# A decoder layer on one core: queries in halves, tile 0's convolution beside attention, side work as one even stream over the prompt rows

## The reference, cut to what matters

```python
mod = silu(c) @ w_ada + b_ada            # sh1, sc1, gt1, sh2, sc2, gt2: six pieces of 1024 columns
h   = rms_norm(x, norm1) * (1 + sc1) + sh1
z   = h @ w_in                           # q, three k/v pairs, branch gates, GLU input
o_attn = nsa(z)                          # compressed, selected and window branches, 8 heads
u   = glu_a * sigmoid(glu_b)             # convolution: 31 taps, 512 channels, then LayerNorm, silu
mix = concat(rms_norm(o_attn), conv(u) * scale) @ w_out
x   = x + gt1 * mix
h2  = rms_norm(x, norm2) * (1 + sc2) + sh2
q   = h2 @ peer_q                        # 8 heads x 2 halves x 128
s   = q . sub_keys                       # 128 scores for each head and half
# per head: top 16 of each half, top 16 of their 256 sums -> 16 expert indices and softmax gates
x   = x + gt2 * sum_k gate_k * gelu(h2 . expert_u[idx_k]) * expert_v[idx_k]
```

## Time and profile before

| | us |
|---|---|
| median of 3 runs | 2302.16 |
| lowest, highest | 2285.15, 2314.85 |
| the profiled execution's own time | 2287.22 |
| its span, first to last instruction | 2285.2 |

### The profile page before, as it was taken

One profiled execution on the slowest core, in us unless ns is written; L12 is line 12 of the kernel. 1 busy time (PEld: TensorE's weight loads), 2 busy tenths in 40 slices (PEclk: granted clock), 3 DMA queues, 4 the chain that ended last, 5 costly groups with the idle time before them and its releaser, 6 DMA issues.

```text
span 2285.2 us, 29811 instructions
## 1 busy us (share of the span) xinstructions
PE 1654.6 (72%) x10176; PEld 979.5 (43%) x10176; DVE 1289.0 (56%) x3724; ACT 656.7 (29%) x1676; POOL 604.9 (26%) x548
## 2 busy tenths in 40 slices
PE   7876358896854769877539798879689858769743
PEld 5746324453621435545116445646254514436300
DVE  1641687565388585743887565327766441443655
ACT  2132133273112433811224275112224220231111
POOL 0000133232323323322423233312323211222342
PEclk9787669697967887988769699889798876675665
DMA  7684789998998899989879999986989866798897
GB/s 283 211 324 145 280 351 426 382 405 360 389 412 325 327 416 385 426 328 426 355 323 390 383 393 399 384 305 224 414 321 410 322 248 217 281 381 320 308 416 296
DMA packets 149256, 782.11 MB, mean 342 GB/s; under 512 B 17303, under 2 KB 53047, under 8 KB 59554
## 3 DMA queue, kind: packets, MB, share of 16 engines
q0 software_dynamic: 78336, 570.46, 62.0%
q1 hardware_dynamic: 70771, 209.77, 24.0%
HBM read 773.75 MB, written 10.99 MB: 343 GB/s over the span
## 4 chain that ended last, share of the span: by engine, by line
PE 39%; DVE 26%; DMA 16%; issue 7%; ACT 6%; SPq 5%; POOL 1%; POOLq 0%; ACTq 0%; DVEq 0%
PE bank L994 13%; DMA expert_rows<-in_expert_uv,expert_index 10%; DVE expert_rows L1837 6%; PE bank L825 6%; DVE conv_out L1447 4%; PE bank L696 4%; PE bank L607 3%; PE bank L800 3%; PE bank L872 2%; DMA gate_or_shift_and_scale<-mod_dram 2%; SPq L1909 2%; DMA weight_units<-in_w_ada_units 2%; PE bank L759 1%; DVE stage_room L1647 1%; DVE stage_room L1636 1%
## 5 line engine op out<-in xcount | busy, mean ns | idle before, releaser
L1866 POOL DMA_INDIRECT expert_rows<-in_expert_uv,expert_index x544 | 604.7, 1111 | 1652.8 <-PE bank L994 1250.8
L994 PE MATMUL bank<-expert_rows,weight_diagonals 64*64 64x512 f32 x4096 | 654.4, 768 | 254.0 <-ACT weight_diagonals L1337 208.0
L1837 DVE CUSTOM_DVE_ANT_0 expert_rows<-expert_rows,h_rows 128x1024 f32<-128x1024 f32 x544 | 657.5, 1220 | 205.7 <-DMA expert_rows<-in_expert_uv,expert_index 203.8
L994 PEld LDWEIGHTS bank<-expert_rows,weight_diagonals 64*64 64x64 f32 x4096 | 160.2, 163 | 569.7 <-ACT weight_diagonals L1337 274.3
L1328 ACT ACTIVATE group_gelu<-group_dots 128x2 f32<-128x2 f32 x272 | 55.2, 203 | 764.7 <-DVE group_dots L1837 720.8
L1337 ACT ACTIVATE weight_diagonals<-consts_sb,group_weights 128x64 f32<-128x64 f32 (+1 forms) x544 | 158.3, 338 | 294.1 <-DVE group_weights L1804 285.9
L825 PEld LDWEIGHTS bank<-stage_room,weight_units 128*128 128x128 f32 x1280 | 169.4, 217 | 41.0 <-issue 37.2
L825 PE MATMUL bank<-stage_room,weight_units 128*128 128x128 f32 (+1 forms) x1280 | 176.8, 301 | 2.4 <-ACT stage_room L1224 2.4
L1804 DVE TENSOR_TENSOR group_weights<-group_gelu,expert_gate 128x2 f32<-128x2 f32 x272 | 43.3, 159 | 195.2 <-ACT group_gelu L1328 178.6
L1447 DVE SCALAR_TENSOR_TENSOR conv_out<-stage_room,small_weights,conv_out 128x128 f32<-128x128 f32 (+1 forms) x600 | 150.4, 322 | 0.0
L872 PE MATMUL bank<-weight_units,prompt_bias 128*128 128x256 f32 x512 | 121.9, 395 | 0.0
(11 more groups left out here) (245 smaller groups left out, 1583.2 us busy)
## 6 DMA issues: line engine op xcount, KB each, us to landing
weight_units<-in_w_in_units SPq DMA_DIRECT2D x45, 1024.0 KB
weight_units<-in_peer_q_units SPq DMA_DIRECT2D x40, 1024.0 KB
weight_units<-in_w_ada_units SPq DMA_DIRECT2D x24, 1024.0 KB
weight_units<-in_w_out_units SPq DMA_DIRECT2D x20, 1024.0 KB
weight_units<-in_w_units SPq DMA_DIRECT2D x16, 1024.0 KB
expert_rows<-in_expert_uv,expert_index POOLq DMA_INDIRECT x544
weight_units<-in_cmp_pages SPq DMA_DIRECT2D x128, 64.0 KB
gate_or_shift_and_scale<-mod_dram SPq DMA_DIRECT2D x12, 512.0 KB
```

The source lines that it names most:

```text
L994: last = mm(e.bank[2 * a + c][o * HD:(o + 1) * HD, :], e.diag[ps, m % (NG * GR)], e.ring[ps, m % RING, cs], start=first, stop=final)
L1837: vec.tensor_tensor_reduce(out=row, in0=row, in1=e.h2[:, i % 2], scale=1.0, scalar=0.0, op0=ALU.mult, op1=ALU.add, accum_out=e.dots[:, q % ...
L1866: pool.indirect_dma_start(e.ring[:, n % RING], None, e.io["expert_uv"], bass.IndirectOffsetOnAxis(ap=e.eidx[:, i % 2, j:j + 1], axis=0)).t ...
```

## The change

- The plan. conv(0) leaves z(0) and stands in one item with att(0) and ada2; its taps come five to a slot for tile 0 (nine elsewhere). ada2 has units 8 to 19; units 20 to 23 (gate 2) become a stage ada3, in one item with topk1(0) among the rows of tile 0. query is cut into query0 (units 0 to 3, then, for prompt tiles, the scores of heads 0 to 3) and query1 (units 4 to 7 and the other scores); topk0 of a prompt tile stands in one item with query1. sc(0) stands alone, sc(1) beside topk1(3), sc(2) and sc(3) follow each other after z(4); SC_LATER goes.
- The spread. `slots_before` takes the items of all windows after window 0 as one list and spreads it over the first 500 rows (512 - 12) evenly. Its lengths add up to 1347; windows 1 and 2 have 290 and 306 of them, and the 12 rows at the end of each tile are no longer left out, except for tile 3's.
- Memory. The keys are loaded in two half units of 0.5 MB, each taking a slot; queries of a prompt tile share one space of 8 heads' halves; scores have a space for each half. ET (the turned probabilities) is sized by tile, so that tile 0's leaves the convolution's input alone. c's columns and the ada partials move to `ysum`, gate 2's bias to `g2`, its rows to `yt`.
- Queues. POOL waits for the first three modulation pieces in DRAM and not for the fourth. `keep_mod(1)` moves to ahead of wo(0,1), and `keep_mod(3)`, gate 2's `mod_rows` and `load_y(0)` to ahead of in(1,8). ACT waits for ada unit 23 before it keeps tile 0's first half.

```diff
-            "mix": (18, 32), "query": (38, 65), "topk0": (31, 27), "topk1": (31, 27), "sc": (42, 32), "satt": (48, 90)}
+            "mix": (18, 32), "query0": (20, 35), "query1": (19, 32), "ada3": (6, 12), "topk0": (31, 27), "topk1": (31, 27), "sc": (42, 32), "satt": (48, 90)}
...
-    return first + body + [("mix", i), ("query", i), ("topk0", i)]
+    last = [("query1", i), ("topk0", i)]
+    return first + body + [("mix", i), ("query0", i)] + (last if i == PT else [tuple(last)])
...
-    windows = [[("ada1", 0), ("x", 0), ("glu", 0), (("z", 0), ("conv", 0)), ("cmp", 0),
-                (("att", 0), ("ada2", 0)), ("mix", 0), ("query", 0), ("topk0", 0)]]
+    windows = [[("ada1", 0), ("x", 0), ("glu", 0), ("z", 0), ("cmp", 0), (("att", 0), ("ada2", 0), ("conv", 0))]
+               + chain_of(0)[-3:]]
...
-    last, then = windows[3].pop(), windows[4].pop(0)
-    windows[3] += [("sc", 0), (last, ("sc", 1))]
-    windows[4] = [(then, ("sc", 2))] + windows[4][:3] + [("sc", 3)] + windows[4][3:]
+    windows[1][0] = (("topk1", 0), ("ada3", 0))
+    windows[3] += [("sc", 0)]
+    windows[4] = [(("topk1", PT - 1), ("sc", 1))] + windows[4][1:4] + [("sc", 2), ("sc", 3)] + windows[4][4:]
...
+    base = sum(slots_of(item) for item in windows[0])
+    ends, done, begun = [0.0], {}, {}
+    for item in (item for w in windows[1:] for item in w):
+        k = slots_of(item)
...
+        ends += [ends[-1] + length_of(item) * (s + 1) / k for s in range(k)]
+    room, before = FIRST[PT] - 12, []
+    for j in range(ROWS):
+        reach = ends[-1] * min(1.0, (j + 1) / room) + 1e-6
+        before.append(sum(1 for x in ends[1:] if x <= reach))
...
+    def scores_of(i, half):
+        keys = key_half(i, half)
+        prod.freed(pe, ("pq", i, 2 * half + 1))
+        for q in range(2):
+            out = prod.open(pe, ("scores", i, 2 * half + q))
+            for a in range(4):
+                last = mm(out[:, a * P:(a + 1) * P], e.q2T[:, 4 * q + a, 0:P], keys[:, 4 * q + a], start=True, stop=True)
+            last.then_inc(prod.ready, 1)
+            if q:
+                units.used_by(("scores", i, 2 * half + 1))
+            yield
...
+        yield from queries(i, range(4))
         if i < PT:
...
+            yield from scores_of(i, 0)
...
+        else:
+            prod.wait(act, ("adaR", 23))
...
-            if n % 9 == 8 and n < 4 * CK - 1:
+            per = 5 if i == 0 else 9
+            if n % per == per - 1 and n < 4 * CK - 1:
...
-    pool.wait_ge(e.s_md[3], 16)
+    for m in range(3):
+        pool.wait_ge(e.s_md[m], 16)
...
-            sp.dma_start(slot, io["keys_unit"]).then_inc(sem, 16)
+            sp.dma_start(slot[:, 0:D], io["keys_unit"][:, key[2] * D:(key[2] + 1) * D]).then_inc(sem, 16)
...
-        if key == ("ada", 22):
+        if key == ("wo", 0, 1):
             keep_mod(1)
         if key == ("wo", 0, 2):
             keep_mod(2)
-        if key == ("pq", 0, 1):
+        if key == ("in", 1, 8):
             keep_mod(3)
+            mod_rows(e.g2, e.s_gl, 3, 0)
+            load_y(0)
```

More of the change, by code:

```diff
@@ L481, in weight_units @@
         "ada1": lambda i: [("ada", u) for u in range(8)],
-        "ada2": lambda i: [("ada", u) for u in range(8, 24)],
+        "ada2": lambda i: [("ada", u) for u in range(8, 20)],
+        "ada3": lambda i: [("ada", u) for u in range(20, 24)],
         "glu": lambda i: [("in", i, 5 + ct) for ct in range(4)],
@@ L486, in weight_units @@
         "mix": lambda i: [("wo", i, q) for q in range(4)],
-        "query": lambda i: [("pq", i, u) for u in range(8)] + [("keys", i)],
+        "query0": lambda i: [("pq", i, u) for u in range(4)] + ([("keys", i, 0)] if i < PT else []),
+        "query1": lambda i: [("pq", i, u) for u in range(4, 8)] + ([("keys", i, 0)] if i == PT else []) + [("keys", i, 1)],
         "sc": lambda part: [("pages", part // 2, part % 2 * 2 + s) for s in range(2)],
@@ L805, in mix, with queries @@
             yield
[L807 removed]
+    def queries(i, us):
         r = rows(i)
[L809 to L818 removed]
+        for u in us:
             w = units.take(("pq", i, u)).rearrange("p (k n) -> p k n", k=KD)
@@ L836, in query, with key_half, query0, query1 @@
             yield
-        keys = units.take(("keys", i)).rearrange("p (a n) -> p a n", a=2 * PH)
-        if i < PT:
-            for q in range(4):
-                prod.freed(pe, ("pq", i, 3))
-                out = prod.open(pe, ("scores", i, q))
-                for a in range(4):
-                    last = mm(out[:, a * P:(a + 1) * P], e.q2T[:, 4 * q + a, 0:r], keys[:, 4 * q + a], start=True, stop=True)
-                last.then_inc(prod.ready, 1)
-                if q == 3:
-                    units.used_by(("scores", i, 3))
-                yield
+    def key_half(i, half):
+        return units.take(("keys", i, half))[:, 0:D].rearrange("p (a n) -> p a n", a=PH)
+    def scores_of(i, half):
[9 more added lines that the diff above has]
+            yield
+    def query0(i):
+        r = rows(i)
+        pe.wait_ge(e.s_h2, i + 1)
+        for q in range(2):
+            out = prod.open(pe, ("h2T", i, q))
+            for k in range(4):
+                last = turn(out[:, k * r:(k + 1) * r], e.h2[0:r, i % 2, (4 * q + k) * P:(4 * q + k + 1) * P],
+                            ident[0:r, 0:r])
+            last.then_inc(prod.ready, 1)
+        yield
+        prod.freed(pe, ("h2T", i, 1))
+        yield from queries(i, range(4))
+        if i < PT:
+            yield from scores_of(i, 0)
+    def query1(i):
+        yield from queries(i, range(4, 8))
+        if i < PT:
+            yield from scores_of(i, 1)
         else:
@@ L967, in satt @@
             last.then_inc(prod.ready, 1)
-    stages = {"ada1": lambda i: ada(range(0, 8)), "ada2": lambda i: ada(range(8, 24)), "x": x, "glu": glu, "z": z,
-              "cmp": cmp, "att": att, "mix": mix, "query": query, "sc": sc, "satt": satt}
+    stages = {"ada1": lambda i: ada(range(0, 8)), "ada2": lambda i: ada(range(8, 20)),
+              "ada3": lambda i: ada(range(20, 24)), "x": x, "glu": glu, "z": z, "cmp": cmp, "att": att, "mix": mix,
+              "query0": query0, "query1": query1, "sc": sc, "satt": satt}
     slots = Slots(side(e.windows, stages), e.before, e.total)
@@ L1218, in mix, with query0 @@
         root(slice(36, 37), r, D).then_inc(e.s_x1q, 1)
-    def query(i):
+    def query0(i):
         r = rows(i)
@@ L1226, in query, with query_half @@
         yield
-        for q in range(4):
+        yield from query_half(i, 0)
+    def query_half(i, half):
+        r = rows(i)
+        for q in range(2 * half, 2 * half + 2):
             for _ in range(8):
@@ L1252, in sc @@
         kv, half = part // 2, part % 2
-        if part == 2:
-            for _ in range(SC_LATER):
-                yield
         act.wait_ge(e.s_h2, PT)
@@ L1304, in satt @@
                 yield
-    stages = {"ada1": lambda i: ada(range(0, 8), True), "ada2": lambda i: ada(range(8, 24), False), "x": x, "glu": glu,
-              "z": z, "cmp": cmp, "att": att, "mix": mix, "query": query, "topk0": lambda i: topk(i, 0),
+    stages = {"ada1": lambda i: ada(range(0, 8), True), "ada2": lambda i: ada(range(8, 20), False),
+              "ada3": lambda i: ada(range(20, 24), False), "x": x, "glu": glu,
+              "z": z, "cmp": cmp, "att": att, "mix": mix, "query0": query0, "query1": lambda i: query_half(i, 1), "topk0": lambda i: topk(i, 0),
               "topk1": lambda i: topk(i, 1), "sc": sc, "satt": satt}
@@ L1688, in sc @@
         crow, csq = e.crow_s, e.csq_s
-        for _ in range(35 + (SC_LATER if part == 2 else 0)):
+        for _ in range(35):
             yield
@@ L1791, in satt @@
                             ).then_inc(prod.free(("srows", g)), 1)
-    stages = {"ada1": lambda i: ada(range(0, 8)), "ada2": lambda i: ada(range(8, 24)), "x": x, "glu": glu, "z": z,
+    stages = {"ada1": lambda i: ada(range(0, 8)), "ada2": lambda i: ada(range(8, 20)),
+              "ada3": lambda i: ada(range(20, 24)), "x": x, "glu": glu, "z": z,
               "conv": conv, "cmp": cmp, "att": att, "mix": mix, "topk0": lambda i: topk(i, 0),
```

116 lines of the change are left out of this document (54 added, 62 removed).

## The result

| | before | changed |
|---|---|---|
| median, us | 2302.74 (4 runs) | 2207.27 (4 runs) |
| lowest, highest | 2285.15, 2314.85 | 2197.89, 2228.35 |
| the profiled execution | 2287.22, span 2285.2 | 2228.35, span 2226.8 |
| ratio | | 0.960, interval 0.951 to 0.970 |

The profiled execution of the changed kernel is the slowest of its four, so a second trace of the same kernel, a1 (2209.02 us, span 2207.4), stands beside it here wherever a term of some us is at stake. Each ratio is to the kernel before on the same chip; where two medians of different chips stand side by side, the text says so.

The account below looks back on a forecast made before the run. Row part bound mostly by DMA of gathers and weights (some 1783 of 2003 us). Prologue -11 and rows -25 gave -36, from the median 2302 to 2266 us; range 2212 to 2320.

Parts of the forecast that it names:

- The spread: Among the rows: 35 rows, 88 us of gathers, move from DMA-bound stretches to late ones, free where DMA idled.
- satt -14: Sample attention: carries 33.4 rows after 28 without getting longer, saving 14 us; bounds 0 and -14.
- the group -13: query(3), topk0(3), sc(0) to sc(2): idle time 33 us in place of 46, so -13; bounds 0 and -25.
- The rule of the Trainium skill: In satt: the issuing engine's sequencer is its own bound, so 172 us stays with 33 rows; otherwise 46 us worse.
- The change of tile: Falls into glu and z, not topk1: -12 before, +5 to +12 now; three times, -14 + 15, about 0.
- topk0 and topk1 now follow each other without the 12 quiet rows between: Tiles 1 and 2: DVE is full in such a stage, so +5 us; bounds 0 and +15.
- query(4): Tile 4's query: PE busy 85 of 85 us, so a row still costs PE time; 3 of 20 us idle won.
- Holds: A second hold of PE on ACT's copy before the scores, one more per prompt tile: 3 x 2 = +6 us.
- Rival B: PE's holds before the scores pass to the gathers: +55 in place of +6, total 2315 us; chance 0.12.
- A: Late stages swallow all 35 moved rows in idle DMA time: -88 in place of -41, total 2219; chance 0.22.
- C: Idle time only moves and the row part stays, but for gate 2: 2296 us; chance 0.23 together with D.
- D: Prologue: attention with conv(0) costs the full +25, halves of query give 8: +14 for -11, 2291; 0.23 with C.

Follow-up runs that it names:

- b1: The changed kernel with conv(0) beside z(0) again, nine taps a slot: 2195.9 us, ratio 0.956 to the kernel before.
- b3: The changed kernel with gate 2's ada units 20 to 23 back in the prologue, beside att(0) with the convolution: 2208.5 us, ratio 0.961.
- b2: The changed kernel with the two DRAM cache copies issued in satt instead of right before the first gather: 2205.4 us, ratio 0.958.
- d1: The changed kernel with satt's planner length 125 in place of 90, so 45 rows beside it in place of 33: 2214.5 us, ratio 0.964.
- a2: The kernel before with only the even spread over 500 rows added, its stages and their order kept: 2267.6 us, ratio 0.988.
- a4: The changed kernel with each tile's topk0 behind query1 instead of beside it, in the prologue and among the rows: 2263.8 us, ratio 0.987.
- a3: The changed kernel with the old spread, window by window with 12 quiet rows: 2259.4 us, ratio 0.986 to the kernel before.
- e1: b1 with PE's LEAD 3 in place of 4: 2252.8 us, ratio 0.988 to the kernel before.

## Why the prediction was wrong

The order of things was right, and some of the terms; the sum missed by 59 us of the medians (95 saved, 36 forecast). By the traces of before and a1, 78 us were saved, so 42 of the 59 can be laid to terms; the other 17 are that medians and profiled executions lie differently. The 42 are: the first row 18 us later than forecast, the idle time 43 us shorter (early 31, from topk1(2) to mix(3) -11, behind satt 17, the rest 6), and the DMA engines' busy time 16 us shorter: 5 are gate 2's, which did not add to the bytes behind the first row, as gathers that landed ahead of that row made up for them; the other 11 nothing here explains. Point by point:

- First gather: 265 forecast, 266.5 measured. z -5.9 (forecast -3), attention +8.7 (+7), halves -14.2 (-15), the rest +1.6. The +7 was held to be partly paid by gate 2's leaving; b1 and b3 show that the convolution's place costs some 10 in all and that gate 2's leaving gives 2 beside it, 5 without it.
- Not foreseen: the copies, moved behind the second half's weights, hold up row 0 for 15 us. It cost nothing that b2 shows, since the DMA engines were full in those 15 us either way.
- The spread, satt -14, the group -13: right. 33 rows in satt at 169 us, idle 51.0 to 37.0; query(3) to the last sc 52.4 to 36.6, and 35 rows taken off the early stages as planned.
- The rule of the Trainium skill weighed there, "Perfetto Trace Analysis", section "What 'DMA-bound' means", gave the right length at 33 rows. But my reading of the track was wrong: it has two holes, 16.5 us and 5.1, not one, and both end with PE's release of a slot (shown with d1), so SP was not the only bound even before. With 45 rows the holes add up to 31 us, and satt grew by 11.
- The change of tile, -14 where it was and +15 where it is: the second half is right in size and came at one change of three. Of a1's three, the one at 1186 has 12.8 us of idle DMA time in the 20 us around PE's wait, the other two none. That one, with topk1(2) and the start of glu (16 us from 1065 to 1105, as much as before), is the excess from topk1(2) to mix(3): 27.1 us where 15 were forecast. There the forecast was 12 us too low, which hid a part of what follows.
- **The step that failed: "topk0 and topk1 now follow each other without the 12 quiet rows between [...] +5", with "+6" for the holds.** Measured in their stretch: idle time 56.5 to 43.7 and, in a1, 34.1, where +9 was forecast. I priced the loss of the quiet rows, which is real (a2, without the pair: +12), and counted the pair of query1 and topk0 only in the prologue and in tile 3's group. In tiles 1 and 2 it puts four weight units under DVE's work, so that topk1 starts with room in the ring of gathered rows: the idle time from h2 to the end of topk1 fell from 37.6 us in the two tiles to 16.9 in a1, and is 38.3 in a4, without the pair. a4 is 58 us slower, of which this is 21.
- **The term that was mis-sized: query(4), "3 us of its 20 idle are won".** All of it was won, 22.2 to 0.6 for mix(4) to topk0(4), and by the spread (a2: 3.9; a3, without it: 17.8). I had read PE busy 85 of 85 us as a bound on what rows cost there. With five rows more PE was busy 69.5 of 75 us at a granted clock of 0.81, and in a2 the first 37.2 us, at 0.59 and with PE busy throughout, had 3.1 us of idle DMA time.
- Holds: +6 forecast, no growth measured; 23.3 us in nine, where seven had 25.2. Rival B had feared two of 11.5 for each tile.

The rivals. A gave 2219, nearer than the forecast, but by luck, not by its mechanism: the late stretches did not swallow 35 rows for nothing. From topk1(2) on they took 30 us longer (1133 to 1163) where free rows would have meant 0 and the forecast's terms 49; most of what A had too much here, the early stages had gained. B is refuted: holds did not grow, and e1, which shortened them, lost over 50. C, the idle time only moves, fits neither part: 59 to 74 us of it are gone. D had the right sign for attention, +9 of its +25, and the wrong one for the halves.

## What to carry to other kernels

A stage that uses no weights gives the DMA engines only gathers to run ahead with, and the ring of gather buffers bounds that. Two such stages in a row fill the ring in the first and idle in the second; set the first beside a stage that uses weights, and both have work for the DMA engines. Cut a trace by the same work, not by the same tile, before comparing, and keep one ledger, idle time of the bounding resource by stretch, with a forecast for each stretch: here it would have shown that no term spoke for the pair in tiles 1 and 2. An engine busy all of a stretch is not yet a bound on what one row more costs there: compare a run that has more rows in it, and read the granted clock beside both.

## What the runs showed of the hardware

- DMA busy time for the same bytes lay between 1770 and 1792 us in all fifteen traces, from the first row on (b2's holds the two copies, 4.4 MB, besides); the total followed mostly the idle time, 139 to 220 us. The 20 us of spread in the busy time stay unexplained.
- Where the DMA engines are full, the order of their work did not matter: with the copies ahead of the first gathers, row 0 was multiplied 21 us after its gather was issued, without them 7, and the end of the program did not move (2205.4 and 2205.9, on two chips).
- query(4), with the rows' products among its own, kept PE busy 85.0 us at a granted clock of 0.59 (20 rows) and 69.5 at 0.81 (25 rows). More rows do not by themselves keep the clock up: with thirteen rows in query0(4), a1 had 0.91, b1 0.75 and a2 0.59.
